# Router logits with tokens in partitions: which side of the matmul is stationary

## The chip, the core and the metric

The kernel runs on one core of a Trainium2 chip. The metric is the device time of one execution in microseconds (us). The core has TensorE (PE in the profile, PEld for its loads of the stationary operand), VectorE (DVE), ScalarE (ACT), GpSimd (POOL) and SyncE (SP), which run side by side and wait for each other through semaphores. TensorE writes to PSUM only; DVE and ACT read PSUM.

## The reference, cut to what matters

Two layers of a transformer-like trunk over 512 latent and 256 context tokens of width 1024; the second layer updates the latent tokens alone. Each layer is a block of token mixers and then a mixture of 16 experts. The router of that mixture is the place of the change:

```python
def grouped_moe(h, router_w, router_b, w1, w3, w2):
    logits = jnp.einsum('bld,de->ble', h, router_w, preferred_element_type=jnp.float32)
    s = jax.nn.sigmoid(logits)
    sb = s + router_b.astype(jnp.float32)
    grp = sb.reshape(sb.shape[:-1] + (N_EXPERT_GROUPS, EXPERTS_PER_GROUP))
    gscore = jnp.sum(lax.top_k(grp, GROUP_SCORE_TOPK)[0], axis=-1)
    gsel = jnp.argmax(gscore, axis=-1)
    ...
    _, idx = lax.top_k(jnp.where(in_group, sb, -jnp.inf), TOP_K)
    ...
    for e in range(N_EXPERTS):
        a = jax.nn.silu(h @ w1[e]) * (h @ w3[e])
        y = y + combine[..., e:e + 1] * (a @ w2[e])
```

`h` is (tokens, 1024), `router_w` is (1024, 16); everything is float32.

## The kernel before, in words

`trunk` writes one program by engine; a loop over the layer `l` holds, for each engine, its part of every stage, and named semaphores (`S(name)`, with the count that `at(name, l, n)` works out for layer `l`) set the order between the engines. `signals` holds how often each name is raised in a layer. `NT` is the number of tiles of 128 tokens: 6 in layer 0, 4 in layer 1. `KD` is 8, the number of 128-wide pieces of the model width; `NE` is 16.

The stretch around the change comes behind the output projection and ahead of the experts. In order:

- DVE writes the normed and modulated rows of a tile, tokens in partitions, to one of three buffers `h2tok` (L1961, L1962), two passes of 1024 columns a tile, and raises `h2_tok`. ACT stores these rows to memory (L1451), from where the experts later gather them.
- PE turns the tile in eight transposes of 128x128 (L997) into the PSUM pair `psb(t % 2)` and raises `h2_tr`. ACT copies the turned tile to `h2T[t % 2]` (L1455) and raises `h2T`. The copy of a tile waits until the logits of the tile two before are done.
- PE, one tile behind the transposes, multiplies: eight steps over the model width into `psb(3)[0:NE, ...]`, the router's weights `rwv` stationary (128 rows, 16 columns), the turned tile moving (128 columns). L1003 is that line. Each such float32 product shows as two matmuls in the trace, so 16 a tile. The logits lie with the experts in 16 partitions and the tokens along the columns.
- When all tiles are done, ACT copies the logits to SBUF (`lgT`, L1457), PE turns them back in `NT` small transposes into `psb(2)` (L1009), and ACT applies the sigmoid from there to `r_s` (L1459), now with the tokens in partitions. `route_sb` and `route_ps` carry these handovers.
- PE runs 45 transposes of the identity into a bank that nobody reads (`awake(3, 45)`, L1013, the line of the instruction is L653), then waits for DVE.
- DVE picks the two experts of each token from `r_s` (L1974 to L2002), PE counts the tokens of each expert (L1016, L1018), 55 more transposes of the identity follow, DVE works out blocks and places (L2015 to L2041), PE turns these into tables (L1027), 60 more transposes follow. With the expert numbers of the blocks (L2049) SP starts to load the experts' weights (L537, L591).
- The experts' blocks follow (L629 and others).

PE, ACT, DVE and SP each take their instructions in the order of the program text, so a wait holds up what stands behind it on the same engine.

Of the kernel before, what the change touches and what calls it, by code (L numbers as in the profile page):

```python
# [22 lines left out]
ACT = mybir.ActivationFunctionType  # L23
AX = mybir.AxisListType

P = 128
# [5 lines left out]
TOK = SEQ + CTX  # L32
LT = SEQ // P
AT = TOK // P
# [6 lines left out]
BC = BW // P  # L41
# [16 lines left out]
NE, NG = 16, 4  # L58
# [63 lines left out]
def signals(name):  # L122

    blocks = expert_blocks(TOK)
    rounds = H * ((2 * AT + 3) // 4)
    once = "g_scaled wT wT_tr"
    by_tile = ("cn cnT cn_tr h2T h2_tok h2_tr hT_hi hT_tile h_tok h_tr lg_ps n1_sq sgv sv_sq t_gain t_hrt t_qk "
               "t_sqd t_ss x_new n1_eps n1_rt pj t_sq t_eps t_rt h_aff")
    by_chunk = "cv_cu po_mix po_pl po_pp sgu_mix sgu_sum sgu_u"
    by_unit = "probs s_ps pv"  # L130
    by_head = "neg_tr neg_row o_sb"
    by_block = "aT_ps aT_sb aT_lo a_sb h1_ps h_ps put sil y_ps y_sb"
    counts = {
        **dict.fromkeys(once.split(), 1), "route": 4, "route_ps": 3, "route_sb": 2, "sum_eps": 2, "sum_rt": 2, **dict.fromkeys(by_tile.split(), AT), **dict.fromkeys(by_chunk.split(), BC),
        **dict.fromkeys(by_unit.split(), H * len(score_units(AT))), **dict.fromkeys(by_head.split(), H),
        **dict.fromkeys(("mx_ps", "negmax"), H * AT), "o_n": BC, **dict.fromkeys(by_block.split(), blocks),
        **dict.fromkeys(("g_prod", "g_ps", "g_sig"), 4 * KD), **dict.fromkeys(("qkT", "qk_hi", "qk_tr"), rounds),
        **dict.fromkeys(("idx", "xT_ps", "xgT", "xg_lo"), blocks + 1), **dict.fromkeys(("m_hi", "m_lo", "n2_sq", "w_sc", "w_tr", "w_x"), KD),
        **dict.fromkeys(("up_ps", "up_sb"), 4 * AT), **dict.fromkeys(("br_hi", "br_lo"), 4 * BC),
        **dict.fromkeys(("w_hi", "w_lo"), SPLITS), "prod": CHUNKS, "cv_evac": 2 * BC, "cv_y": BC, "po_pad": 1,  # L140

        "h2_st0": 16 * (AT // 3), "h2_st1": 16 * (AT // 3), "h2_st2": 16 * (AT // 3), "par_b": 16 * 2, "par_g": 32, "par_w": 16 * 3, "par_n2": 48,
        "par_g2": 16, "par_p": 16, "par_sb": 32, "x_back": 16 * AT,
        "xg0": 16 * (blocks // 2 + 1), "xg1": 16 * ((blocks + 1) // 2),
        "y_st0": 16 * ((blocks + 1) // 2), "y_st1": 16 * (blocks // 2), **{f"yg{j}": 32 * YPAIR.count(j) for j in range(3)},
    }
    return counts[name]
# [27 lines left out]
def trunk(nc, A, out):  # L175
# [6 lines left out]
    with ExitStack() as ctx:  # L182
# [20 lines left out]
        MGZ = place("MGZ", 2 * KD * TOK)  # L203
# [15 lines left out]
        ident = place("ident", P)  # L219
# [14 lines left out]
        def W(l):  # L234
            return TOK if l < DEPTH - 1 else SEQ
# [65 lines left out]
        def psb(i):  # L301
            return ps[:, i, :]
# [68 lines left out]
        h2T = [late[:, j * D:(j + 1) * D].rearrange("p (k t) -> p k t", k=KD) for j in range(2)]  # L371
# [37 lines left out]
        eid_i = place("eid_i", MAXB + 1, I32)  # L409
        tab_i = place("tab_i", MAXB + 1, I32)  # L410
        idx_i = [place(f"idx_i{j}", 1, I32) for j in range(2)]
        lgT = MGZ[0:NE, 0:TOK]

        NB = MAXB + 1
        ge_blk = MGZ[:, 0:2 * AT * (NB + 1)].rearrange("p (k t b) -> p k t b", k=2, t=AT)
# [6 lines left out]
        rwv = rw[:, :].rearrange("p (k e) -> p k e", k=KD)  # L422
# [18 lines left out]
        def S(name):  # L441
            if name not in sems:
                sems[name] = ctx.enter_context(nc.semaphore(name))
            return sems[name]

        def at(name, l, n):

            return n + (signals(name) if l else 0)
# [173 lines left out]
        def _(pe):  # L622
            mm = pe.matmul
# [43 lines left out]
            for l in range(DEPTH):  # L667
                NT = tiles(l)
# [59 lines left out]
                if l == 0:  # L728
                    pe.wait_ge(S("mod_row"), 1)
                    for k in range(KD):  # L730
# [3 lines left out]
                        for j in range(4):  # L734
                            last = mm(bank(4)[32 * j:32 * j + 2, 0:512], c_vec[:, k, :], mod_slot(k)[:, j * 512:(j + 1) * 512],
                                      start=(k == 0), stop=(k == KD - 1))
# [3 lines left out]
                for c in range(4):  # L740
                    last = pe.transpose(bank(7)[:, c * P:(c + 1) * P], mod_first[:, c * P:(c + 1) * P], ident[:, :])
# [161 lines left out]
                for j in range(4):  # L903
                    pe.wait_ge(S("w_lo"), split_no(l, S_V + j))
                    w = [a.rearrange("p (k n) -> p k n", n=BW) for a in parts(S_V + j, 2 * BW)]
                    for t in range(NT):
                        for i in range(2):
                            k, tok = 2 * j + i, slice(t * P, (t + 1) * P)
                            last = three(bank(t), (hH[:, k, tok], hL[:, k, tok]), (w[0][:, i, :], w[1][:, i, :]),
                                         BW, k == 0, k == KD - 1)  # L910
# [8 lines left out]
                for g in range(BC):  # L919
                    pe.wait_ge(S("sgu_u"), at("sgu_u", l, g + 1))  # L920
                    for t in range(NT):
                        last = mm(psb(home[g])[:, t * P:(t + 1) * P], sgv[:, t, g * P:(g + 1) * P], sguwT[:, g, :],
                                  start=True, stop=True)
# [5 lines left out]
                for c in range(BC):  # L929
                    for j in range(3):  # L930
# [8 lines left out]
                        last = chunk(l, S_CV + w, (hH, hL), w % 4)  # L939
                        if l == 0 and S_CV + w in rows_after:  # L940
                            last = half_turn(rows_after[S_CV + w], w % 4)
# [6 lines left out]
                for g in range(BC + 1):  # L948
# [9 lines left out]
                    if g >= 1:  # L958
# [4 lines left out]
                        last = mm(psb(2 + h % 2)[:, 0:SEQ], poolw[:, BC - 1 - h, :], pooled[h % 2][:, 0:SEQ], start=True, stop=True)  # L963
                        if W(l) > SEQ:
                            last = mm(psb(2 + h % 2)[:, SEQ:TOK], poolw[:, BC - 1 - h, :], pooled[h % 2][:, SEQ:TOK], start=True, stop=True)
# [7 lines left out]
                for n in range(KD + 1):  # L973
# [5 lines left out]
                    if n >= 1:  # L979
# [4 lines left out]
                        for t in range(NT):  # L984
                            last = pe.transpose(psb(2 + m % 2)[:, t * P:(t + 1) * P], wsc[m % 2][:, t * P:(t + 1) * P], ident[:, :])
# [5 lines left out]
                for t in range(NT + 1):  # L991
                    if t < NT:
                        pe.wait_ge(S("h2_tok"), at("h2_tok", l, t + 1))
                        if t >= 2:
                            pe.wait_ge(S("h2T"), at("h2T", l, t - 1))
                        for k in range(KD):
                            last = pe.transpose(psb(t % 2)[:, k * P:(k + 1) * P], h2tok[t % 3][:, k * P:(k + 1) * P], ident[:, :])  # L997
                        last.then_inc(S("h2_tr"), 1)
                    if t >= 1:
                        u = t - 1  # L1000
                        pe.wait_ge(S("h2T"), at("h2T", l, u + 1))
                        for k in range(KD):
                            last = mm(psb(3)[0:NE, u * P:(u + 1) * P], rwv[:, k, :], h2T[u % 2][:, k, :],  # L1003
                                      start=(k == 0), stop=(k == KD - 1))
                        last.then_inc(S("lg_ps"), 1)

                pe.wait_ge(S("route_sb"), at("route_sb", l, 1))
                for t in range(NT):
                    last = pe.transpose(psb(2)[:, t * NE:(t + 1) * NE], lgT[:, t * P:(t + 1) * P], ident[0:NE, 0:NE])  # L1009
                last.then_inc(S("route_ps"), 1)  # L1010


                awake(3, 45)  # L1013
                pe.wait_ge(S("route"), at("route", l, 1))
# [2 lines left out]
                for t in range(NT):  # L1017
                    last = mm(rank[:, t + 1:NT + 1, :], ones[:, :], r_any[:, t:t + 1, :].to_broadcast([P, NT - t, NE]),  # L1018
                              start=False, stop=(t == NT - 1))
# [5 lines left out]
                for i in range(2 * NT):  # L1025
                    k, t = i // NT, i % NT
                    last = mm(psb(3)[:, 0:2 * (nb + 1)].rearrange("p (s b) -> p s b", s=2), at_place[:, k, t, :],  # L1027
                              tab_blk[:, k, t, :, 0:nb + 1],
                              start=(i == 0), stop=(i == 2 * NT - 1))
# [73 lines left out]
        def _(act):  # L1103
            act_f = act.activation
# [20 lines left out]
            for l in range(DEPTH):  # L1125
                NT = tiles(l)
# [263 lines left out]
                for g in range(BC + 1):  # L1390
                    if g < BC:
# [3 lines left out]
                        last = act_f(pp[g % 2][:, PLL:PLL + SEQ], psb(g % 2)[:, 0:SEQ], ACT.Copy)  # L1395
                        if W(l) > SEQ:
                            last = act_f(pp[g % 2][:, PLC:PLC + CTX], psb(g % 2)[:, SEQ:TOK], ACT.Copy)
# [32 lines left out]
                for n in range(KD):  # L1430
# [4 lines left out]
                    last = act_f(wsc[n % 2][:, 0:SEQ], psb(n % 2)[:, 0:SEQ], ACT.Copy, scale=cw[:, g:g + 1])  # L1435
                    if W(l) > SEQ:
                        last = act_f(wsc[n % 2][:, SEQ:TOK], psb(n % 2)[:, SEQ:TOK], ACT.Copy, scale=cw[:, g + KD:g + KD + 1])
# [16 lines left out]
                        act.wait_ge(S("lg_ps"), at("lg_ps", l, t - 1))  # L1454
                    act_f(h2T[t % 2], psb(t % 2).rearrange("p (k t) -> p k t", k=KD), ACT.Copy).then_inc(S("h2T"), 1)  # L1455
                act.wait_ge(S("lg_ps"), at("lg_ps", l, NT))
                act_f(lgT[:, 0:W(l)], psb(3)[0:NE, 0:W(l)], ACT.Copy).then_inc(S("route_sb"), 1)  # L1457
                act.wait_ge(S("route_ps"), at("route_ps", l, 1))
                act_f(r_s[:, 0:NT, :], psb(2)[:, 0:NT * NE].rearrange("p (t e) -> p t e", t=NT), ACT.Sigmoid)\  # L1459
                    .then_inc(S("route_sb"), 1)  # L1460
                table(ACT.Silu)
# [78 lines left out]
        def _(dve):  # L1540
# [13 lines left out]
            for l in range(DEPTH):  # L1554
                NT = tiles(l)
# [304 lines left out]
                for c in range(BC):  # L1860
# [20 lines left out]
                    for a, b, o in cstreams:  # L1881
                        z = cvy[c % 2][:, o:o + b - a]
                        last = tt(z, z, gbs[c % 2][:, a:b], ALU.mult)
# [85 lines left out]

                    return a[:, :, None].to_broadcast([P, a.shape[1], n])  # L1970

                dve.wait_ge(S("route_sb"), at("route_sb", l, 2))
                dve.wait_ge(S("const"), 10)
                link(tt(sbv, s, rbias[:, None, :].to_broadcast([P, NT, NE]), ALU.add))  # L1974
                g3 = sbv.rearrange("p t (g e) -> p (t g) e", g=NG)
# [34 lines left out]
                    tt(gw[k][:, 0:NT], gw[k][:, 0:NT], r_den[:, 0:NT], ALU.mult)  # L2010

                nb = expert_blocks(W(l))
                dve.wait_ge(S("route_ps"), at("route_ps", l, 2))
                cnt = psb(2)[:, NT * NE:(NT + 1) * NE]
                link(tt(r_cnt, cnt[:, :, None].to_broadcast([P, NE, 6]), steps6[:, None, :].to_broadcast([P, NE, 6]), ALU.is_gt))  # L2015
                link(dve.tensor_reduce(r_nb, r_cnt, AX.X, ALU.add))
# [30 lines left out]
                link(dve.tensor_reduce(r_eid[:, 0:nb], blk, AX.X, ALU.add))  # L2047
                link(ts(r_eid[:, 0:nb], r_eid[:, 0:nb], float(NE - 1), None, ALU.min))
                cp(eid_i[:, 0:nb], r_eid[:, 0:nb]).then_inc(S("route"), 1)  # L2049
                dve.wait_ge(S("route_ps"), at("route_ps", l, 3))  # L2050
                code = psb(3)[:, 0:nb + 1]
                skip, half, dst = (a[:, 0:nb + 1] for a in (r_skip, r_half, r_dst))
                ts(half, code, YROWS + 0.5, float(-YROWS), ALU.is_gt, ALU.mult)
# [302 lines left out]
```

## Time and profile before

| | |
|---|---|
| Median of 3 runs | 2384.25 us (2383.99 to 2386.27) |
| Profiled execution | 2390.06 us, its span 2388.3 us |
| PE busy | 2142.1 us (90% of the span) |
| PE's weight loads busy | 1734.2 us (73%) |
| DVE, ACT, POOL busy | 1373.4, 992.8, 368.7 us |
| Granted PE clock, mean | 0.941 |
| The stretch of the change | about 1035 to 1056 us (layer 0), 2080 to 2096 us (layer 1) |

The span is the time from the first to the last instruction that the profiler shows; the execution's own time is 1.8 us longer, and lies 5.8 us above the median of the runs. The granted clock is the share of 2.4 GHz that TensorE was given; it has two levels in this trace, 1.00 and 0.50 (2.4 and 1.2 GHz). Matmuls overlap: the duration of one is longer than the distance to the next, so the cost of a sequence is read from the starts (or from the span of a group divided by its count), not from durations.

### The profile page before, as it was taken

How to read it: one execution, taken by the hardware profiler on the slowest of the kernel's cores; microseconds unless marked ns; L12 is line 12 of the kernel's file. 1: busy time of each engine (PE TensorE's matmuls, PEld its weight loads, DVE VectorE, ACT ScalarE, POOL GpSimd, SP SyncE). 2: the span in 40 equal slices, each digit the busy share in tenths (PEclk: the TensorE clock that was granted, in tenths of full speed). 3: DMA queues.
4: the chain of work that ended last, by engine and by line, in shares of the span. 5: the costliest groups of instructions: out<-in, count | busy, mean ns of one | idle time of the engine just before them, and what ended most of it. 6: DMA issues, size and time to landing. Idle time of an engine off the chain costs nothing.

```text
span 2388.3 us, 28736 instructions
## 1 busy us (share of the span) xinstructions
PE 2142.1 (90%) x10673; PEld 1734.2 (73%) x10673; DVE 1373.4 (58%) x1496; ACT 992.8 (42%) x1290; POOL 368.7 (15%) x400
## 2 busy tenths in 40 slices
PE   5879999899979999978999866999999989889994
PEld 3556787788768888867878654667788767778783
DVE  2646554755765433266888666453333454559885
ACT  3645412211211222225888655442422222338883
POOL 3300000000000001003555423000000000015552
PEclk7989999999989999998999987999999999999997
DMA  7020144444654232119999552003334343269994
GB/s 271 1 62 1 32 133 133 112 118 129 193 165 146 58 119 75 41 74 338 389 371 375 187 199 70 1 1 84 93 77 114 85 131 115 73 223 356 370 369 149
DMA packets 247398, 360.00 MB, mean 151 GB/s; under 512 B 22528, under 2 KB 180480, under 8 KB 245760
## 3 DMA queue, kind: packets, MB, share of 16 engines
q1 hardware_dynamic: 219776, 297.65, 38.2%
q0 software_dynamic: 22336, 42.07, 5.0%
q10 hardware_dynamic: 5184, 18.88, 2.0%
q8 instruction: 70, 1.15, 0.2%
q14 instruction: 32, 0.26, 0.0%
HBM read 354.23 MB, written 36.78 MB: 164 GB/s over the span
## 4 chain that ended last, share of the span: by engine, by line
PE 72%; DVE 11%; DMA 8%; ACT 5%; issue 3%; SPq 1%; POOL 0%; DVEq 0%; ACTq 0%; POOLq 0%
PE ps L639 33%; PE ps L629 17%; PE ps L641 8%; DMA RING<-in_moe_w 4%; PE ps L862 3%; DMA MGZ<-in_mod_w 2%; PE ps L1038 1%; PE ps L821 1%; PE ps L846 1%; PE ps L847 1%; DVE WS L1711 1%; PE ps L848 1%; ACT HTH L1484 1%; PE ps L810 1%; PE ps L1003 1%
## 5 line engine op out<-in xcount | busy, mean ns | idle before, releaser
L639 PE MATMUL ps<-HTH,WS 128*128 128x512 f32 x1664 | 587.4, 400 | 31.4 <-DVE WS L1711 13.2
L639 PEld LDWEIGHTS ps<-HTH,WS 128*128 128x128 f32 x1664 | 317.2, 191 | 109.6 <-issue 15.2
L639 PE MATMUL ps<-HTL,WS 128*128 128x512 f32 x832 | 330.2, 397 | 0.0
L629 PE MATMUL ps<-HTH,MGH 128*128 128x512 f32 x1000 | 283.4, 407 | 13.2 <-DVE MGH L2069 13.2
L1269 ACT ACTIVATE WS<-RAWB 128x1024 fp32r<-128x1024 f32 (+1 forms) x128 | 162.7, 1272 | 292.3 <-PE ps L641 97.0
L1711 DVE TENSOR_TENSOR WS<-RAWB,WS 128x1024 fp32r<-128x1024 f32 (+1 forms) x128 | 190.6, 1489 | 158.4 <-ACT WS L1269 158.3
L629 PE MATMUL ps<-HTL,MGH 128*128 128x512 f32 x800 | 232.4, 403 | 9.4 <-DVE HTL L2079 9.4
L641 PE MATMUL ps<-HTH,WS 128*128 128x256 f32 x832 | 235.7, 283 | 0.0
L629 PEld LDWEIGHTS ps<-HTH,MGH 128*128 128x128 f32 x1000 | 190.8, 195 | 55.8 <-DVE MGH L2069 8.9
L1484 ACT ACTIVATE HTH<-RING 128x2048 fp32r<-128x2048 f32 x100 | 191.2, 1912 | 82.3 <-DMA RING<-in_moe_w 59.3
L639 PE MATMUL ps<-BRH,WS 128*128 128x512 f32 x512 | 183.4, 397 | 16.9 <-DVE BRL L1857 13.3
L639 PEld LDWEIGHTS ps<-HTL,WS 128*128 128x128 f32 x832 | 159.0, 191 | 36.5 <-issue 1.0
L629 PEld LDWEIGHTS ps<-HTL,MGH 128*128 128x128 f32 x800 | 149.7, 192 | 39.5 <-issue 9.7
L1754 DVE TENSOR_TENSOR T<-T,ps 128x768 f32<-128x768 f32 (+1 forms) x48 | 39.4, 821 | 228.6 <-PE ps L641 116.8
L1287 ACT ACTIVATE T<-ps 128x768 f32<-128x768 f32 (+1 forms) x64 | 45.1, 705 | 294.5 <-PE ps L641 183.1
L1723 DVE SCALAR_TENSOR_TENSOR MGZ<-MGZ,scP 128x1024 f32<-128x1024 f32 x112 | 139.1, 1280 | 42.2 <-DMA MGZ<-in_mod_w 41.2
L641 PEld LDWEIGHTS ps<-HTH,WS 128*128 128x128 f32 x832 | 159.9, 192 | 0.1
L2079 DVE TENSOR_TENSOR HTH<-RING,HTH 128x2048 fp32r<-128x2048 f32 x50 | 114.6, 2293 | 54.0 <-ACT HTH L1484 51.9
L2079 DVE TENSOR_TENSOR HTL<-RING,HTH 128x2048 fp32r<-128x2048 f32 x50 | 114.6, 2292 | 23.6 <-ACT HTH L1484 23.6
L639 PEld LDWEIGHTS ps<-BRH,WS 128*128 128x128 f32 x512 | 97.2, 190 | 40.2 <-DVE BRL L1857 14.0
L641 PE MATMUL ps<-HTL,WS 128*128 128x256 f32 x416 | 117.8, 283 | 0.0
L2079 DVE TENSOR_TENSOR HTL<-RING,HTL 128x2048 fp32r<-128x2048 f32 x50 | 114.2, 2283 | 5.7 <-ACT HTL L1490 5.7
(336 smaller groups left out, 3775.1 us busy)
## 6 DMA issues: line engine op xcount, KB each, us to landing
RING<-in_moe_w SPq DMA_DIRECT2D x300, 512.0 KB
RAWB<-in_w_in SPq DMA_DIRECT2D x112, 512.0 KB, 4.3
MGZ<-in_mod_w SPq DMA_DIRECT2D x80, 512.0 KB, 4.1
RAWB<-in_w_branch SPq DMA_DIRECT2D x64, 256.0 KB, 4.7
MGZ<-y_rows POOLq DMA_DIRECT2D x20, 512.0 KB, 6.8
RAWB<-in_w_o SPq DMA_DIRECT2D x16, 512.0 KB, 3.9
HTF<-in_mod_w SPq DMA_DIRECT2D x6, 1024.0 KB
h_rows<-BR ACTq DMA_DIRECT2D x10, 512.0 KB, 2.6
```

The source lines that it names most:

```text
L629: last = mm(out, a, b, start=(first and i == 0), stop=(stop and i == 2))
L639: last = mm(psb(pair)[:, 0:SEQ], a[:, k0 + k, :], b[:, k, 0:SEQ], start=go, stop=end)
L641: last = mm(psb(pair)[:, SEQ:TOK], a[:, k0 + k, :], b[:, k, SEQ:TOK], start=go, stop=end)
L810: last = pe.transpose(head_bank[0 if h else r][0:QK, (i % 4) * P:(i % 4 + 1) * P], src, ident[:, :])
L862: last = mm(bank(4 + h % 2), v_tile(u)[:, h // 2, v0:v0 + P], pt, start=(u == 0), stop=(u == AT - 1))
L1269: act_f(parts(s, words(s))[0], raw_slab(r, words(s)), ACT.Copy).then_inc(S("w_hi"), 1)
L1287: act_f(sig[u % 2][:, 0:W(l)], psb(u % 2)[:, 0:W(l)], ACT.Sigmoid).then_inc(S("g_sig"), 1)
L1484: act_f(up_hi[half], slot(n % SLOTS), ACT.Copy).then_inc(S("e_hi"), 1)
L1711: tt(lo, raw_slab(FIRST + s, words(s)), hi.bitcast(F32), ALU.subtract).then_inc(S("w_lo"), 1)
L1723: stt(acc, half_slot(n), c, acc, ALU.mult, ALU.add).then_inc(S("half_acc"), 1)
L1754: link(tt(prod[:, 0:W(l)], sig[u % 2][:, 0:W(l)], psb(2 + u % 2)[:, 0:W(l)], ALU.mult))
L2079: tt(lo, slot(n % SLOTS), hi.bitcast(F32), ALU.subtract).then_inc(S("e_lo"), 1)
```

## The change

The sides of the router's product are swapped. The turned tile is the stationary operand (128 columns, the tokens), the sixteen columns of the router's weights move, and the result lands in `psb(2)` with the tokens in partitions, 16 columns a tile. The copy L1457 with its buffer `lgT`, the back turns L1009 and the waits between them are gone. The sigmoid reads `psb(2)` as before. The counts of `route_sb` and `route_ps` go down by one each.

```diff
-        "route": 4, "route_ps": 3, "route_sb": 2,
+        "route": 4, "route_ps": 2, "route_sb": 1,
...
                         for k in range(KD):
-                            last = mm(psb(3)[0:NE, u * P:(u + 1) * P], rwv[:, k, :], h2T[u % 2][:, k, :],
+                            last = mm(psb(2)[:, u * NE:(u + 1) * NE], h2T[u % 2][:, k, :], rwv[:, k, :],
                                       start=(k == 0), stop=(k == KD - 1))
                         last.then_inc(S("lg_ps"), 1)
-
-                pe.wait_ge(S("route_sb"), at("route_sb", l, 1))
-                for t in range(NT):
-                    last = pe.transpose(psb(2)[:, t * NE:(t + 1) * NE], lgT[:, t * P:(t + 1) * P], ident[0:NE, 0:NE])
-                last.then_inc(S("route_ps"), 1)
...
                 act.wait_ge(S("lg_ps"), at("lg_ps", l, NT))
-                act_f(lgT[:, 0:W(l)], psb(3)[0:NE, 0:W(l)], ACT.Copy).then_inc(S("route_sb"), 1)
-                act.wait_ge(S("route_ps"), at("route_ps", l, 1))
                 act_f(r_s[:, 0:NT, :], psb(2)[:, 0:NT * NE].rearrange("p (t e) -> p t e", t=NT), ACT.Sigmoid)\
                     .then_inc(S("route_sb"), 1)
...
-                dve.wait_ge(S("route_sb"), at("route_sb", l, 2))
+                dve.wait_ge(S("route_sb"), at("route_sb", l, 1))
...
-                dve.wait_ge(S("route_ps"), at("route_ps", l, 2))
+                dve.wait_ge(S("route_ps"), at("route_ps", l, 1))
...
-                dve.wait_ge(S("route_ps"), at("route_ps", l, 3))
+                dve.wait_ge(S("route_ps"), at("route_ps", l, 2))
```

## Rows read from the trace of the kernel before

**Rows 1.** The page: its chain by engine; and the router's group among the PE lines.
```profile
span 2388.3 us, 28736 instructions
...
PE 72%; DVE 11%; DMA 8%; ACT 5%; issue 3%; SPq 1%; POOL 0%; DVEq 0%; ACTq 0%; POOLq 0%
...
L1003 PE MATMUL ps<-MGZ,rw 128*16 128x128 f32 x160 | 19.6, 279 | 0.0
```

**Rows 2.** Chain of waits, layer 0: start us, us, what; then ACT's wait.
```profile
1046.69 1.02 PE ps L997 x8
1047.72 1.85 PE ps L1003 x16
1049.57 1.02 PE ps L997 x8
1050.59 3.61 PE ps L1003 x32
1054.22 0.81 ACT MGZ L1457
1055.08 0.56 PE ps L1009 x6
1055.66 0.26 ACT BR L1459
...
1082.34 1.93 ACT L1484 ACTIVATE HTH<-RING 128x2048 fp32r<-128x2048 f32 x1 [24.92 <-DMA RING<-in_moe_w]
```

**Rows 3.** Timeline of the tile loop, layer 0: start us, us, engine, line.
```profile
1043.61 1.23 DVE L1962 TENSOR_TENSOR BR<-BR,HTF 128x1024 f32<-128x1024 f32 x1
1046.06 1.23 DVE L1962 TENSOR_TENSOR BR<-BR,HTF 128x1024 f32<-128x1024 f32 x1
1046.62 0.85 PEld L997 LDWEIGHTS ps<-ident,BR 128*128 128x128 f32 x8 [0.21 <-issue]
1047.76 1.02 ACT L1455 ACTIVATE MGZ<-ps 128x1024 f32<-128x1024 f32 x1 [1.85 <-PE ps L997]
1049.50 0.85 PEld L997 LDWEIGHTS ps<-ident,BR 128*128 128x128 f32 x8 [0.21 <-issue]
1050.52 3.38 PEld L1003 LDWEIGHTS ps<-MGZ,rw 128*16 128x16 f32 x32 [0.17 <-issue]
```

**Rows 4.** Timeline of layer 1 behind the last logits.
```profile
2095.13 0.59 ACT L1457 ACTIVATE MGZ<-ps 16x512 f32<-16x512 f32 x1 [2.57 <-PE ps L1003]
...
2096.22 0.22 ACT L1459 ACTIVATE BR<-ps 128x64 f32<-128x64 f32 x1 [0.51 <-PE ps L1009]
```

**Rows 5.** Timeline and groups by shape: few moving columns behind 128 stationary ones.
```profile
1062.68 1.42 PEld L1018 LDWEIGHTS ps<-BR,ones 128*128 128x128 f32 x12
2110.10 1.86 PEld L1027 LDWEIGHTS ps<-MGZ 128*128 128x128 f32 x16 [0.66 <-DVE MGZ L2041]
...
L1018 PE MATMUL ps<-BR,ones 128*128 128x96 f32 x2 | 0.4, 268 | 0.0
L1018 PE MATMUL ps<-BR,ones 128*128 128x16 f32 x1 | 0.3, 262 | 0.0
```

**Rows 6.** Timeline, layer 1: eight transposes at the lower clock.
```profile
2083.06 1.57 PEld L997 LDWEIGHTS ps<-ident,BR 128*128 128x128 f32 x8 [0.82 <-DVE BR L1962]
```

**Rows 7.** Windows: length; PE, PEld, DVE, ACT, POOL busy; granted clock; DMA.
```profile
1035.00:1038.50 3.50, 2.92 (x13) 2.55 (x14) 3.46 (x4) 1.02 (x1) 0.00 (x0) 0.50 0.42 171
1038.50:1042.00 3.50, 3.50 (x30) 2.78 (x29) 3.43 (x4) 1.02 (x1) 0.00 (x0) 0.99 0.67 272
1069.30:1072.70 3.40, 1.65 (x15) 1.41 (x14) 3.33 (x8) 0.00 (x0) 0.00 (x0) 1.00 0.00 0
1072.70:1076.10 3.40, 3.40 (x18) 3.40 (x18) 0.76 (x3) 0.00 (x0) 0.00 (x0) 0.50 0.16 42
1076.10:1079.50 3.40, 3.40 (x18) 3.40 (x18) 0.84 (x6) 0.00 (x0) 0.92 (x1) 0.50 0.82 229
1714.40:1717.80 3.40, 1.38 (x13) 1.19 (x11) 3.37 (x4) 0.44 (x1) 0.00 (x0) 1.00 0.24 45
1717.80:1721.20 3.40, 2.49 (x6) 2.02 (x7) 3.23 (x6) 1.21 (x3) 0.00 (x0) 0.50 0.74 214
2083.00:2086.40 3.40, 3.34 (x15) 2.58 (x16) 3.37 (x4) 1.72 (x2) 0.00 (x0) 0.50 0.41 166
2086.40:2089.80 3.40, 3.40 (x31) 2.77 (x29) 1.48 (x2) 1.02 (x1) 0.00 (x0) 0.99 0.44 180
```

**Rows 8.** Timeline: PE at the counting matmuls, layer 0 and layer 1.
```profile
1062.46 0.47 PE L1016 MATMUL ps<-BR,tri 128*128 128x112 f32 x2 [1.78 <-DVE BR L2002]
2102.34 0.45 PE L1016 MATMUL ps<-BR,tri 128*128 128x80 f32 x2 [1.10 <-DVE BR L2002]
```

More of the change, by code:

```diff
@@ L133, in signals @@
     counts = {
-        **dict.fromkeys(once.split(), 1), "route": 4, "route_ps": 3, "route_sb": 2, "sum_eps": 2, "sum_rt": 2, **dict.fromkeys(by_tile.split(), AT), **dict.fromkeys(by_chunk.split(), BC),
+        **dict.fromkeys(once.split(), 1), "route": 4, "route_ps": 2, "route_sb": 1, "sum_eps": 2, "sum_rt": 2, **dict.fromkeys(by_tile.split(), AT), **dict.fromkeys(by_chunk.split(), BC),
         **dict.fromkeys(by_unit.split(), H * len(score_units(AT))), **dict.fromkeys(by_head.split(), H),
@@ L411, in trunk @@
         idx_i = [place(f"idx_i{j}", 1, I32) for j in range(2)]
-        lgT = MGZ[0:NE, 0:TOK]
         NB = MAXB + 1
```

## The prediction

> **What bounds the kernel now.** I read the page first. TensorE (PE) carries 72% of the chain that ended last, and the group the change rewrites, the router matmuls of L1003, is 160 instructions and 19.6 us of PE time in a span of 2388.3 us [rows 1]. So the change can't be worth much by its own work. What decides is whether the router sits on the path, and what its matmuls do beside computing. The chain of waits says that it is on the path, in both layers [rows 2]: transposes of L997 (8 a tile), router matmuls of L1003 (16 a tile, each of the 8 k steps being two instructions), again transposes, without another engine between them; then ACT's copy (L1457), the ten back turns (L1009, six of them here), ACT's sigmoid (L1459), some seven us of DVE work, the read of the expert numbers on SP, and a wait for the experts' weights from memory. These weights are asked for only when DVE has finished the routing, and ACT sits idle for 24.92 us until they land. So a microsecond more or less before the sigmoid is a microsecond at the end; nothing behind it can take it up.
>
> In layer 0 the loop's period is 2.87 us (1046.62 to 1049.50), PE's own: 8 transposes and 16 matmuls, in which PE is always at work. DVE needs 2.45 us for a tile (1043.61 to 1046.06), ACT's copy 1.02 us. So PE is the bound of this loop, by 0.4 us a tile [rows 3].
>
> **Removed.** The copy L1457, the back turns L1009 and the two handovers. From the copy's start to the sigmoid's start: 1055.66 - 1054.22 = 1.44 us in layer 0 [rows 2], 2096.22 - 2095.13 = 1.09 us in layer 1 [rows 4]. What follows is late by nothing else: the sigmoid waits for the logits alone, and ACT's function table for it is called for before the loop. Gain 2.53 us, all on the path. DVE's waits only change their numbers. The logits go to the PSUM pair from which the sigmoid read before, and the 45 transposes that keep PE awake (L1013) start as soon as the last logits are issued; that costs the sigmoid nothing.
>
> **Changed: the router matmul with its sides swapped.** Before, the stationary tile has 16 columns and 128 columns move; after, 128 are stationary and 16 move. Count stays 16 a tile. Before, 32 of them take 3.38 us of weight loads, (3.38 - 0.10) / 31 = 0.106 us each [rows 3]. What a matmul with few moving columns behind a full stationary tile costs is shown by L1018: its twelve move 96, 80, 64, 48, 32 and 16 columns, two of each, and take (1.42 - 0.19) / 11 = 0.111 us each, with the same duration at 96 columns (268 ns) as at 16 (262 ns). L1027 gives (1.86 - 0.19) / 15 = 0.111 us at 48 columns [rows 5]. The spacing follows the stationary load, not the columns that move. With the clock as before the loop thus gets 0.005 us x 16 = 0.08 us a tile dearer, 0.8 us over the ten tiles. Bounds: 0.106 (no loss) and 0.128 (the chain's 1.02 us for eight L997 transposes behind a full stationary tile, handover included [rows 2]; +3.5 us over the ten tiles); I take 0.111, since L1018 has the very shape.
>
> The Trainium skill (TensorE: Matmul & The Clock Gate, "LDWEIGHTS (loading the stationary operand)") says that the load's time goes by the number of stationary columns, whatever the rows; that agrees in kind with the rows. Its "Back-to-back issue gap" would let a warm matmul of up to 64 columns follow after some 25 ns; by that alone the sixteen would take 0.4 us a tile, and the rows of L1018 speak against it.
>
> **Changed: what PE does between the transposes.** This is the term that I think decides. PE's clock has two levels, 2.4 GHz (granted 1.00) and 1.2 GHz (0.50). At the lower one a transpose costs (1.57 - 0.23) / 7 = 0.191 us instead of 0.107, and L1027's matmuls 3.40 / 18 = 0.19 us instead of 0.111 [rows 6, 7]. Where the clock turns is seen in the windows [rows 7]. It is at 0.50 when the loop starts in both layers, since PE idles before. In layer 0 it is up at 1038.5, after thirteen transposes. In layer 1 it is up at 2086.4, after eight transposes and some eight router matmuls of 128 columns. At about 1072.7 it falls, after transposes, a pause and the first L1027 matmuls. And then comes the telling stretch: from 1072.7 to 1076.1 PE issues 18 matmuls of L1027, full stationary tile, 56 moving columns, with PE and its weight load busy for 3.40 of 3.40 us, and the clock stays at 0.50. It is up at 1079.5, after a stretch filled mostly with transposes of 128 columns, at the same rate of 18. A PE that is never idle, but loads much and streams little, didn't get its clock back; L922 adds that thirteen 128-column matmuls and then a pause let it fall [rows 7]. After the change two thirds of the loop are matmuls that stream 16 columns behind a full load, a third is transposes. I expect that the clock falls soon after 1042 and, once down, stays down until the 45 transposes: at the low clock the loop streams less still.
>
> The skill's page says (same page, "Part 4: PE-mode transpose") that transposes don't count as PE being busy and don't bring the full clock. The row of 1038.5 contradicts it: nothing but transposes had run. By that rule the clock would fall yet sooner, with the same end.
>
> **The price of the low clock.** Layer 0: mm(0) still runs at the high clock; four tiles of transposes and five of matmuls don't. 32 x (0.191 - 0.107) = 2.7 us and 80 x (0.191 - 0.106) = 6.8 us: 9.5 us, and 0.08 for mm(0), less 1.44: +8.1 us. Layer 1: the trace of before has half of mm(0), two tiles of transposes and three of matmuls at the high clock: 8 x 0.085 + 16 x 0.084 + 48 x 0.085 = 6.1 us, less 1.09: +5.0; should the clock still come up for one tile (16 x 0.08 + 8 x 0.084 = 2.0), +3.0. I take +4.0. The keep-awake transposes start cold: seventeen or so at 0.191, the rest at 0.109, is 17 x 0.191 + 28 x 0.109 = 6.3 us, up to 7.5 if the rise comes later. They hide under the time from the sigmoid's start to L1016: 1062.46 - 1055.66 = 6.8 us in layer 0 and 2102.34 - 2096.22 = 6.1 us in layer 1 [rows 2, 4, 8]. Late by 0 to 0.7 and 0.2 to 1.4: +0.5 in all. PE is ahead of that in both cases today, with 1.78 and 1.10 us to spare [rows 8].
>
> Sum: 8.1 + 4.0 + 0.5 = +12.6 us. The profiled execution took 2390.06 us (span 2388.3, 1.8 us around it); 2402.7 for such a one. The median of the runs, 2384.25, lies 5.8 us lower: 2396.8.
>
> **Rivals.**
> (a) The clock holds. PE has no pause in the loop, and the transposes, at the high clock, may be enough. Then the end is 2.53 - 0.8 = 1.7 us earlier: 2382.5, not slower. It decides at the second tile: if the granted clock is 1.00 from 1042 to the sigmoid, this case holds. For it: in the loop of before the matmul had only 16 stationary columns and the clock still held; against it: L1027's stretch. The skill's page ("Why this matters for your kernels") asks for a PE kept busy without gaps, and by that rule the clock holds, since the loop has none; that would be this case.
> (b) The clock falls in one layer only, or comes back within the loop. Layer 0 alone: 8.1 - 1.0 = +7, 2391; layer 1 alone: 4.0 - 1.4 = +2.6, 2387.
> (c) The matmuls really become cheap. Then DVE is the bound, with 2.45 us a tile: the last h2 tile is there at 1047.3, transposes and copy end by 1049.6, logits by 1050.2 instead of 1054.2: -4 us, in layer 1 as much, with the 2.5 about -11: 2373. L1018 speaks against it.
> (d) The swap does not reach the path, because something beside it holds the routing (the store of h2 rows, the weights): no change, 2384. The chain shows no such wait.
>
> **Chances.** Forecast (low clock in both layers) 0.70, (a) 0.15, (b) 0.10, (c) 0.03, (d) 0.02. A measurement of this kernel can tell about 0.2%, 4.8 us, from no change. Faster: (c), 0.03. Same: (a), (d) and a part of (b), 0.21. Slower: 0.76. The likeliest case by itself spans 2393 (the fall one tile later, 8.1 - 2.0; layer 1 at +3.0; no late transposes: +9) to 2401 (layer 0 never rises, +1.4; layer 1 +5.0; 2.0 late: +16.5). It holds 0.70 at most, so the range goes down over (b) to (a): 2381.6 to 2401.
>
> **What would show it.** Granted clock 0.50 from about 1042 to the 45 transposes in layer 0, and through the loop of layer 1; period of the loop near 5 us instead of 2.87; weight loads of the router matmul 0.11 us apart while the clock is high and 0.19 when it is low; sigmoid directly behind the last logits, some 8 us later than before in layer 0; everything behind it shifted, not stretched. I would be wrong if the clock holds with 16 moving columns, that is if the load of a full stationary tile keeps it up.

## Result, and the profile after

Beside the kernel before, the first four executions of the changed kernel had a median of 2404.85 us (2398.26 to 2408.86) against 2384.8 us (2383.99 to 2386.27): ratio 1.0075, 95% interval 1.0052 to 1.0097. The change makes the kernel slower, by more than was forecast and past the end of the range.

The profiled execution took 2398.26 us, with a span of 2396.5 us. The page's first part and the two groups of the loop, from the profile of the changed kernel:

```profile
span 2396.5 us, 28714 instructions
...
PE 2156.0 (90%) x10663; PEld 1750.9 (73%) x10663; DVE 1373.2 (57%) x1496; ACT 991.8 (41%) x1288; POOL 372.9 (16%) x400
...
L1002 PE MATMUL ps<-rw,MGZ 128*128 128x16 f32 x160 | 32.0, 351 | 0.0
L996 PE MATMUL ps<-ident,BR 128*128 128x128 f32 x80 | 18.6, 410 | 15.0 <-DVE BR L1953 15.0
```

The router's line (L1002 now) stands at 32.0 us of PE time instead of 19.6 [rows 1], though it has the same 160 instructions. The chain of waits in layer 0 shows where (start us, us, what):

```profile
1041.34 0.92 PE ps L996 x8
1042.26 2.52 PE ps L1002 x16
1044.78 1.79 PE ps L996 x8
1046.57 3.23 PE ps L1002 x16
1049.79 1.79 PE ps L996 x8
1051.58 3.23 PE ps L1002 x16
1054.81 1.79 PE ps L996 x8
1056.59 6.65 PE ps L1002 x32
1063.55 0.27 DVE BR L1965
```

It is the chain of [rows 2] with the same links: transposes, router matmuls, transposes. But a tile takes 5.0 us (1044.78 to 1049.79) instead of 2.87, from the fourth tile's transposes on. The copy and the back turns are gone; DVE starts 0.3 us after the last matmul, with only ACT's sigmoid (at 1063.27) between them. The granted clock of that stretch is in the windows (length; PE, PEld, DVE, ACT, POOL busy; clock; DMA share and GB/s):

```profile
1035.50:1038.90 3.40, 2.98 (x14) 2.58 (x14) 3.33 (x4) 1.02 (x1) 0.00 (x0) 0.50 0.50 202
1039.80:1042.90 3.10, 3.10 (x30) 3.10 (x30) 3.07 (x4) 1.51 (x2) 0.00 (x0) 1.00 0.44 165
1043.00:1047.00 4.00, 4.00 (x21) 4.00 (x20) 3.92 (x4) 0.72 (x2) 0.00 (x0) 0.50 0.34 138
1059.00:1062.80 3.80, 3.80 (x19) 3.80 (x20) 0.00 (x0) 0.00 (x0) 0.00 (x0) 0.50 0.00 0
2101.00:2105.00 4.00, 4.00 (x21) 4.00 (x20) 0.00 (x0) 0.00 (x0) 0.00 (x0) 0.50 0.00 0
```

From 1043 to 1062.8, and again in layer 1 (last row), PE and its loads are busy for the whole of each window, and the clock is at 0.50. In [rows 7] it was at 0.99 from 1038.5 and 2086.4 on.

For all kernels below I took the same three marks from the timeline, each counted from the first tile's first transpose: start of the sigmoid, start of the counting matmuls (L1016 before), and the cast of the expert numbers (L2049 before), which SP waits for. A group of matmuls starts with its first weight load. The names in brackets are those of the runs. In the kernel before, layer 0: 1035.13 (first transpose), 1055.66, 1062.46 and 1073.35, so 20.53, 27.33 and 38.22.

| Kernel | layer 0: sigmoid, counting, numbers | layer 1: the same | loss at the numbers, both layers | median minus before |
|---|---|---|---|---|
| before | 20.53, 27.33, 38.22 | 15.55, 21.67, 30.65 | | |
| before, second trace (before_again) | 20.69, 27.50, 38.39 | 15.42, 21.54, 30.51 | 0.0 | 0.8 |
| changed | 27.96, 34.76, 45.64 | 21.07, 28.39, 37.24 | 14.0 | 20.1 |
| changed, second trace (after_again) | 31.09, 37.89, 48.78 | 21.07, 28.21, 37.08 | 17.0 | 15.7 |
| 128 columns (wide128) | 19.60, 26.40, 38.40 | 13.88, 20.01, 28.97 | -1.5 | -0.2 |
| 64 columns (wide64) | 21.13, 27.92, 38.81 | 15.73, 21.85, 30.82 | 0.8 | 2.0 |
| 32 columns (wide32) | 31.12, 37.92, 48.81 | 21.10, 28.48, 37.34 | 17.3 | 13.4 |
| changed, filled pause (after_pre) | 27.14, 33.94, 44.83 | 21.07, 28.36, 37.21 | 13.2 | 12.6 |
| 128 columns in layer 1 only (wide_l1) | 24.83, 31.63, 42.53 | 14.05, 20.18, 29.16 | 2.8 | 9.2 |
| 128 columns, filled pause (wide128_pre) | 19.38, 26.18, 38.19 | 14.05, 20.18, 29.15 | -1.5 | -3.7 |
| the same, longer keep-awake (wide128_long) | 19.38, 26.18, 37.08 | 14.06, 20.18, 29.15 | -2.6 | -2.2 |
| changed, 8 more transposes a tile (fill8) | 22.29, 29.10, 40.00 | 26.09, 32.77, 41.63 | 12.8 | 18.2 |
| the same, filled pause (fill8_pre) | 22.34, 29.74, 40.63 | 18.08, 24.21, 33.19 | 5.0 | 4.0 |

The last column compares medians of one job. The marks are of one execution, the medians of 4 to 12, and the executions of one and the same kernel lie far apart: 93 of the kernel before, over five jobs, went from 2373.44 to 2398.00 us with a median of 2386.4, and the twelve of wide128_pre, in one job, from 2370.38 to 2395.18. That is why the table's marks carry the argument, and the medians only confirm its size.

The traced executions show this too. Both of before lie above its median (2390.06 and 2390.45 us), both of the changed kernel below its own (2398.26 and 2398.13), so their times differ by 8 us where the marks differ by 14.0 and 17.0. What lies outside the two marked stretches took 2319.4 and 2319.8 us in the former, 2313.6 and 2310.5 in the latter, and 2311.9 to 2319.3 in the nine other traces. Whether the routing's delay is in part taken up there can't be told from traces that scatter so. The medians, 15.7 us apart in the larger sample, don't suggest it.

### The profile page after: what moved, and what is told of

Read it like the earlier page. It is cut to its first block, busy times and chain, and to the rows that moved or that the text cites. A ratio compares the mean times of both kernels' runs of the same rounds, so it can differ in the third digit from the quotient of the medians.

```text
span 2396.5 us, 28714 instructions
## 1 busy us (share of the span) xinstructions
PE 2156.0 (90%) x10663; PEld 1750.9 (73%) x10663; DVE 1373.2 (57%) x1496; ACT 991.8 (41%) x1288; POOL 372.9 (16%) x400
## 3 DMA queue, kind: packets, MB, share of 16 engines
q8 instruction: 70, 1.15, 0.2%
## 4 chain that ended last, share of the span: by engine, by line
PE 72%; DVE 11%; DMA 9%; ACT 5%; issue 3%; SPq 1%; POOL 0%; DVEq 0%; ACTq 0%; POOLq 0%
PE ps L638 32%; PE ps L628 15%; PE ps L640 8%; DMA RING<-in_moe_w 4%; PE ps L861 3%; DMA MGZ<-in_mod_w 3%; PE ps L1002 1%; PE ps L1031 1%; PE ps L820 1%; PE ps L718 1%; DVE WS L1702 1%; PE ps L845 1%; PE ps L846 1%; PE ps L847 1%; PE ps L809 1%
## 5 line engine op out<-in xcount | busy, mean ns | idle before, releaser
L628 PE MATMUL ps<-HTH,MGH 128*128 128x512 f32 x1000 | 278.2, 400 | 12.7 <-DVE MGH L2060 11.9
```

The lines of the kernel that those rows point to most:

```text
L628: last = mm(out, a, b, start=(first and i == 0), stop=(stop and i == 2))
```

## Experiments

**The changed kernel again, and the kernel before again.** No edit.

> The changed kernel, unaltered, for a second trace and more times. Theory (the clock falls in the tile loop of both layers): the granted clock is 0.50 from the third or fourth tile to the keep-awake transposes in layer 0 and through the loop of layer 1, whatever the exact moment; sigmoid 6 to 9.5 us after that of before in layer 0 and some 5.5 us more in layer 1; median within 2398 to 2409. Open: the first trace shows some 14 us of loss in the two loops, the median of the runs 20; if that rest has a place, a trace of a slower execution shows it, either in the loops (clock never up in layer 0: 1.4 us more) or in a later stage.

Measured: 2400.37 us (7 executions, 2395.48 to 2407.63), ratio 1.0064 [1.0039, 1.0088], inside the forecast. The sigmoid of layer 0 came later than the 6 to 9.5 us that were forecast, by the case that was left open. Here the clock never came up in layer 0; PE alone in windows of its trace (length, PE busy, clock, DMA):

```profile
1036.00:1040.00 4.00, 4.00 (x20) 0.50 0.54 210
1040.00:1044.00 4.00, 4.00 (x21) 0.50 0.20 76
...
1060.00:1064.00 4.00, 4.00 (x20) 0.50 0.00 0
1064.00:1068.00 4.00, 4.00 (x23) 0.59 0.02 4
1068.00:1072.00 4.00, 3.46 (x32) 1.00 0.01 2
```

It rises only within the keep-awake transposes, which start at 1064.26. The sigmoid comes after 31.09 us, 10.6 later than before; the sigmoid of layer 1 repeats the first trace to the hundredth (21.07). So the loss varies with whether the clock comes up once at the start of layer 0: 14.0 and 17.0 us in the two traces. The seven executions here lie 15.7 us above the thirty of before in the same job, between the two. All eleven of the changed kernel have a median of 2401.05 us, so the 20 us of the first four look like a high draw; the two traces show no third place of loss, but neither is of one of the longest executions.

> The kernel before, unaltered, for a second trace. Its two loops should differ from the first trace's only by how long the start runs at the low clock: 19.5 to 21.5 us from first transpose to sigmoid in layer 0, 14.5 to 16.5 in layer 1, and the clock never falls inside them.

Measured: as expected, and the marks of the two traces of before differ by less than 0.2 us. Both traced executions took nearly the same time (2390.06 and 2390.45 us), so this doesn't say whether the spread between executions lies in this stage. In this job the fifteen others of before had a median of 2390.05 us, 5 above that of the first two jobs.

**The same matmul with 128, 64 and 32 moving columns.** The sixteen columns are read eight, four or two times over; loads, count, and the missing copy and back turns stay as in the changed kernel:

```diff
-                            last = mm(psb(2)[:, u * NE:(u + 1) * NE], h2T[u % 2][:, k, :], rwv[:, k, :],
+                            last = mm(psb(2)[:, u * P:u * P + 128].rearrange("p (c e) -> p c e", e=NE), h2T[u % 2][:, k, :],
+                                      rwv[:, k:k + 1, :].to_broadcast([P, 8, NE]),
                                       start=(k == 0), stop=(k == KD - 1))
```

This is the 128-column form. The sigmoid reads the first sixteen columns of each tile at their new places (that line is not shown).

> The changed kernel with one thing altered: the router's sixteen columns are read eight times over, so 128 columns move behind the same full stationary load; the same 16 instructions a tile, the same results in the first sixteen columns of each tile, copy and back turns still gone. Theory (few moving columns let the clock fall): clock at 1.00 through the loops once it is up, loop period 2.8 to 2.9 us, median 1 to 3 us below before, 2382 to 2384. Rival 1 (the full stationary load of 128 columns is what costs, by itself): the period stays near 5 us and the time near 2400. Rival 2 (the missing copy and back turns change something later, such as the DMA pattern or the keep-awake transposes): the loops are as fast as before, and yet the time stays 5 us or more above before.

> As wide128, with 64 moving columns (sixteen, four times over). Theory: spacing of the router's matmuls unchanged at 0.11 us while the clock is high; whether the clock holds is what is asked. If it holds, 2382 to 2385; if it falls, 2395 or more. The rival of the stationary load gives the same 2400 for 16, 64 and 128 columns.

> The changed kernel with 32 moving columns (the sixteen read twice). With 16 columns the clock fell and stayed down in both traces, with 64 and 128 it came up and held. Theory (few columns behind a full load let it fall): 32 columns are near 16, so the layer-0 loop from first transpose to sigmoid takes 27 to 31 us and the time is 2395 to 2401. Rival (anything above 16 holds the clock): 19.5 to 21 us for that loop and 2384 to 2388.

Measured: 2384.44 us for 128 (ratio 0.9994 [0.9978, 1.0011]), 2386.62 for 64 (1.0007 [0.9991, 1.0022]), 2399.24 for 32 (1.0059 [1.0034, 1.0084]). The times of 128 and 64 are 0.4 and 1.6 us above their forecasts and can't be told from before. Windows of PE in layer 0, first of 128 columns, then of 64, then two of 32 columns (one for each layer):

```profile
1032.50:1036.00 3.50, 3.08 (x14) 0.50 0.51 205
1036.00:1039.00 3.00, 3.00 (x18) 0.56 0.63 247
1039.20:1043.00 3.80, 3.80 (x37) 1.00 0.39 154
1043.00:1047.00 4.00, 4.00 (x39) 1.00 0.44 179
```
```profile
1040.40:1044.40 4.00, 4.00 (x22) 0.50 0.48 186
1044.40:1047.60 3.20, 3.20 (x22) 0.67 0.29 120
1047.70:1051.70 4.00, 4.00 (x40) 1.00 0.40 163
```
```profile
1044.00:1048.00 4.00, 4.00 (x21) 0.50 0.34 138
2093.00:2097.00 4.00, 4.00 (x21) 0.50 0.32 131
```

With 128 and 64 the clock comes up in the loop and stays; with 32 it stays at 0.50 like with 16 (31.12 us to the sigmoid, against 31.09). The stationary load is the same in all four. So the first rival, that the full load costs by itself, falls, and so does the second, that something behind the loop costs: wide128 lacks copy and back turns too. Nor is it the form of the edit, the repeated reading or the new places of the results, since the 32-column kernel has both and is as slow as the changed one. Adding columns whose results nobody reads makes the kernel 15.9 us faster than the changed one in the same job. The number of moving columns is the cause; each width has one trace, and the medians of 12, 12 and 6 executions agree with it.

The weight loads of the 128-column kernel, layer 0, also show what the swap does at the high clock:

```profile
1041.87 0.91 PEld L996 LDWEIGHTS ps<-ident,BR 128*128 128x128 f32 x8
1042.75 1.86 PEld L1002 LDWEIGHTS ps<-rw,MGZ 128*128 128x128 f32 x16
1044.53 0.91 PEld L996 LDWEIGHTS ps<-ident,BR 128*128 128x128 f32 x8
```

Period 2.66 us, not 2.87 (the forecast for this kernel was 2.8 to 2.9): the idle 0.17 and 0.21 us that stood before each group in [rows 3] are gone now that both kinds have 128 stationary columns. The sixteen are (1.86 - 0.19) / 15 = 0.111 us apart, as L1018 had said.

**Starting the loop at the high clock.** 55 transposes of the identity in PE's pause ahead of the tile loop:

```diff
+                awake(3, 55)
                 pe.wait_ge(S("w_x"), at("w_x", l, KD))
                 for t in range(NT + 1):
```

> The changed kernel, 16 moving columns, with 55 transposes of the identity ahead of the tile loop in both layers. Theory: the loop starts at the high clock and loses it within one or two tiles though PE is never idle; the last tiles run at 5.0 us each as before. First transpose to sigmoid 25 to 28 us in layer 0, 17 to 20 in layer 1; time 2392 to 2399. Rival (the clock only never came up, because the loop starts after a pause): clock 1.00 through the loops, 19 to 20 us in layer 0, time 2381 to 2384.

Measured: 2398.49 us (ratio 1.0045 [1.0024, 1.0067]). PE in layer 0:

```profile
1032.00:1036.00 4.00, 2.62 (x25) 1.00 0.55 163
1036.00:1040.00 4.00, 2.70 (x24) 1.00 0.54 220
1040.00:1042.80 2.80, 2.80 (x28) 0.98 0.59 238
1043.00:1047.00 4.00, 4.00 (x21) 0.50 0.32 131
```

The clock is at 1.00 when the loop starts and falls at about 1042.7, in the second tile's router matmuls, with PE busy without a gap from 1039 on. In layer 0 it isn't that the clock never got up; the loop loses it. Layer 1 is another case (PE alone):

```profile
2080.00:2084.00 4.00, 1.95 (x16) 0.97 0.33 132
2084.00:2088.00 4.00, 4.00 (x21) 0.50 0.59 240
```

There the clock falls at about 2083.7, where the second tile's transposes start behind PE's wait for DVE, and before the first router matmul (its load starts at 2085.24). The filled pause bought nothing: 21.07 us to the sigmoid, as in the changed kernel, where 17 to 20 were forecast. What the narrow matmuls do in layer 1 is to keep the clock from coming up again, which with 128 columns it does.

**One layer at a time.** 128 columns in layer 1 only (`if l == 1`), 16 in layer 0.

> The changed kernel with 128 moving columns in layer 1 alone, 16 in layer 0. Theory (a loss in each loop, 7.4 to 10.6 us in layer 0 and 6.4 to 6.6 in layer 1 up to the expert numbers, and nothing elsewhere): 7 to 11 us above before, 2392 to 2396, with layer 1 as in wide128 and layer 0 as in the changed kernel. Rival (the rest of the loss, that the first median showed beyond the two loops, has another place): more than 2398 although layer 1 is whole again.

Measured: 2395.06 us, ratio 1.0038 [1.0022, 1.0055], 9.2 above before. Layer 1 is that of the 128-column kernel (29.16 against 28.97). Layer 0 lost 4.3 us in this trace, since the clock held into the third tile's matmuls there. The median lies within the forecast and agrees with the two layers' loss being separate; the rival, more than 2398, is out.

**More streaming, 16 columns kept.** Eight transposes of the identity behind each tile's router matmuls, so that PE has more to do:

```diff
                         last.then_inc(S("lg_ps"), 1)
+                        if t < NT:
+                            awake(7, 8)
```

> The changed kernel, 16 moving columns, with eight transposes of the identity (128 columns, result unread) behind the router's matmuls of each tile, so PE has half as much again to do per tile. Theory (the clock needs columns that stream): once up, the clock holds, the period is 2.66 + 8 x 0.107 = 3.5 us instead of 5.0, layer 0 from first transpose to sigmoid takes 23 to 26 us, and the kernel is faster for the added work: 2388 to 2395. Rival (the sixteen-column matmul is itself slow, whatever runs beside it): each tile costs its 5.0 us and eight transposes more, over 32 us, and the time is above 2405.

Measured: 2408.26 us beside 2390.05, ratio 1.0096 [1.0060, 1.0132]. The forecast of the time was wrong. Of layer 0 the clock and the period came as forecast, and the sigmoid after 22.29 us, earlier than 23 to 26. PE in both layers of the one trace:

```profile
1044.00:1048.00 4.00, 4.00 (x39) 1.00 0.45 178
1056.00:1060.00 4.00, 4.00 (x39) 1.00 0.01 4
2088.00:2092.00 4.00, 4.00 (x22) 0.50 0.20 80
2100.00:2104.00 4.00, 4.00 (x21) 0.50 0.00 0
```

The same mix holds the high clock in layer 0, at 3.49 us a tile with half as much again to do, and sixteen 16-column matmuls are 0.111 us apart there ((1.86 - 0.19) / 15). So the 16-column matmul is not slow by itself. In layer 1 the mix never got the clock up, and each tile took 6.7 us. To ask whether the state at the start decides, the pause was filled here too:

> fill8 with 55 transposes of the identity in the pause ahead of the loop, so that the loop starts at the high clock in both layers. In fill8's trace the same mix of work held the high clock in layer 0 (period 3.49 us) and never got it up in layer 1 (period 6.7 us). Theory (the mix can hold the clock but not raise it; the state at the loop's start decides): now both layers hold it, periods 3.49 us, last logits 22 us after the first transpose in layer 0 and 15 in layer 1, time 2386 to 2392 beside a before of 2385. Rival (layer 1 differs for another reason): layer 1 stays at 0.50 and 6.7 us a tile, 25.9 us to the last logits, time above 2396.

Measured: 2391.66 us beside 2387.63, ratio 1.0031 [1.0000, 1.0061]. The time is inside the forecast, at its end. Layer 0 held until about 1056.5, in the last tile's router matmuls, some 1.3 us before the sigmoid; the keep-awake transposes then started at the low clock, and the expert numbers came 0.6 us later than in fill8. In layer 1 the clock fell in the first tiles, where PE still waits for DVE, and came up again inside the loop:

```profile
2076.00:2080.00 4.00, 2.00 (x17) 1.00 0.35 141
2080.00:2084.00 4.00, 3.96 (x21) 0.57 0.50 204
2084.00:2088.00 4.00, 4.00 (x24) 0.58 0.16 62
2088.00:2092.00 4.00, 4.00 (x39) 1.00 0.32 131
```

So the clock can come up in this mix and fall in it, against the theory as it was put. What decided in fill8's layer 1 stays open.

**A version that beats both?** 128 columns with the filled pause, and then with longer keep-awake stretches behind it (58 and 68 transposes instead of 45 and 55 in layer 0, 52 and 58 in layer 1):

> wide128 with 55 transposes of the identity in the PE pause of 7.6 us ahead of the tile loop, in both layers. Theory (PE is the loop's bound and starts it at the low clock): the first tiles run at the high clock; the first two are bounded by DVE, so little comes of it in layer 0 (about 0.5 us), about 1 to 1.5 us in layer 1, where the clock came up only within the third tile: 2380 to 2383. Rival (the clock comes up anyway before PE is the bound): no difference to wide128 within 1 us.

> wide128_pre with the keep-awake transposes that follow it made longer, 58 and 68 instead of 45 and 55 in layer 0, 52 and 58 in layer 1. In wide128 and wide128_pre the clock fell to 0.50 in the pause ahead of the counting matmuls in layer 0, and the expert numbers came 1.1 us later for it (12.0 us instead of 10.9 after the counting started). Theory: with the pause filled the counting runs at the high clock: 1 us less than wide128_pre in layer 0, 2379 to 2382. Rival (the transposes are now too long and hold up the counting): counting matmuls later than 26.5 us after the first transpose.

Measured: 2380.99 us (ratio 0.9986 [0.9963, 1.0008]) and 2383.72 us (0.9991 [0.9976, 1.0006]), the second above its forecast of 2379 to 2382. The filled pause moved the sigmoid of layer 0 by 0.22 us and layer 1 not at all (14.05 against 13.88), so the rival of wide128_pre was right. The loop did start at 1.00, but in both layers the clock fell at the second tile's transposes, behind PE's wait for DVE, and came up again inside the loop. PE in layer 1:

```profile
2076.00:2080.00 4.00, 3.25 (x30) 1.00 0.35 142
2080.00:2084.00 4.00, 2.70 (x15) 0.70 0.63 254
2088.00:2092.00 4.00, 4.00 (x38) 1.00 0.30 119
```

In wide128 and wide128_pre the clock was low at the counting matmuls of layer 0, and in wide128_long it was not; wide128 first, then wide128_long:

```profile
1058.96 2.52 PEld L1011 LDWEIGHTS ps<-BR,ones 128*128 128x128 f32 x12
```
```profile
1061.17 1.42 PEld L1012 LDWEIGHTS ps<-BR,ones 128*128 128x128 f32 x12
```

That gives the 1.1 us back (numbers at 37.08 instead of 38.19), and by its marks the kernel is 2.6 us ahead of before. Its interval includes 1.0: no version here is shown to be faster than before.

## Why the prediction was right or wrong

**The mechanism was right.** The router is on the path, and within the routing nothing takes up a delay: the counting follows the sigmoid by 6.80 us in layer 0 of both kernels, and in layer 0 the cast follows the counting by 10.89 and 10.88 us. The clock fell, the period near 5 us came (5.01), and the 128-column kernel shows that the few columns were what did it. Rival (a) held in neither trace of the changed kernel; (b) in neither; (c) is out, the spacing at the high clock is 0.111 us; (d) is out, the delay reaches the expert numbers in both layers.

**The removed part** was sized right in kind: in wide128 the sigmoid comes 0.93 us earlier in layer 0 and 1.67 in layer 1 (1.15 and 1.49 in wide128_long), where 1.44 - 0.48 and 1.09 - 0.32 were the sum with the dearer matmul. How late the clock comes up in each trace is in these numbers as well. A smaller step that failed is "the loop thus gets 0.08 us a tile dearer": the loop at the high clock got 0.21 us a tile cheaper, and the pauses between the groups went. The lower bound, 0.106 us an instruction, was no bound, because the gain lay between the groups.

**The price of the low clock was too small.** This is the step that failed, in two terms: layer 1, taken at +4.0 with at most 5.0, and the case "layer 0 never rises, +1.4".
- The matmul at the low clock was put at 0.19 us, from 18 instructions in a window of 3.40 us of [rows 7]. A window's count includes those that only reach into it. From starts and ends it is 0.214 us: sixteen loads in 3.54, the last of 0.333 us, (3.54 - 0.333) / 15:

```profile
1051.16 3.54 PEld L1002 LDWEIGHTS ps<-rw,MGZ 128*128 128x128 f32 x16
1054.43 1.76 PEld L996 LDWEIGHTS ps<-ident,BR 128*128 128x128 f32 x8
1056.17 6.95 PEld L1002 LDWEIGHTS ps<-rw,MGZ 128*128 128x128 f32 x32
```

  The transposes' 0.191 us was too low as well. The first two loads of a group behind a pause start only 0.06 us apart, and (1.57 - 0.23) / 7 of [rows 6] averages that in; from the second on the same group's loads start 0.213 us apart (2083.12 to 2084.40, six steps). The error is small in the sum, since the high clock's loop was underpriced too: a tile costs 5.01 - 2.87 = 2.14 us more, where 8 x 0.084 + 16 x 0.085 = 2.0 was reckoned, and the last 32 matmuls (1056.17 to 1062.86, against 3.6 us) 3.1 more instead of 2.7.
- Layer 0 was put at +8.1 with the clock up for mm(0). The first trace has +7.4 at the sigmoid, with the clock up a little longer. The second trace has +10.6: the clock never came up. The prediction knew this case ("layer 0 never rises, +1.4") and sized it at half: without it being up, mm(0), a group of transposes and half of mm(1) are at the low clock too, 3.1 us more than in the first trace.
- Layer 1 was put at +4.0, between 3.0 and 5.0. It is +5.5 at the sigmoid in both traces; the rise for one tile, for which 1 us was taken off, never came.
- The late keep-awake transposes were put at +0.5. They cost nothing in layer 0 and 1.2 us in layer 1 (counting 7.32 us behind the sigmoid instead of 6.12), within the stated 0.2 to 1.4.

Together 14.0 and 17.0 us at the expert numbers instead of 12.6, layer 1 with 6.6 and 6.4 of it; the 17.0 lie past the 16.5 from which the range's end was made. That is 1.4 to 4.4 of the 7.5 us by which the measured 20.05 us exceeds 12.6. **The rest is not located.** The range gave the scatter of the kernel itself no room: three executions of before within 2.3 us were taken as its spread, where 93 cover 25 us. With 15.7 us, the difference of the larger sample, the time would have been 2400 and inside. So the traces show that layer 1 lost more than forecast in both, and layer 0 in the second; that the median of four lay 3.85 us past the range's end looks to be in part the draw.

The sentence on the Trainium skill's rule (TensorE: Matmul & The Clock Gate, "Part 4: PE-mode transpose"), that transposes don't bring the full clock, is contradicted again: in the second trace of the changed kernel the clock rises from 0.50 to 1.00 in a stretch that holds nothing but transposes (1064.26 to 1070.7). The other rule that was weighed, of the same page ("Why this matters for your kernels"), that a PE kept busy without gaps keeps its clock, fails in layer 0 of the changed kernel: PE was busy for 3.10 of 3.10 us at 1.00 up to 1042.90 and for 4.00 of 4.00 us from 1043.00 on, and lost it between the two.

## What to carry to other kernels

Before swapping the sides of a small float32 matmul, count what streams as well as what is loaded: behind a full stationary load, few moving columns cost as much as many here (0.111 us each at 16 and at 128), and they may let TensorE's clock fall, or not come up, for everything around them. Where the moving side is narrow, reading it several times over cost nothing at the high clock and kept that clock in this loop (64 and 128 columns did, 16 and 32 didn't). Read the cost of a sequence from starts, never from a window's count, and give the range of a time the scatter of the kernel itself.

## What the runs showed that was not expected

- With 128 stationary columns in both, the groups follow each other without the 0.17 and 0.21 us pauses that stood between a 128-wide and a 16-wide group; the period at the high clock is 2.66 us instead of 2.87. That the unlike widths cause the pauses is likely and was not tried by itself.
- The same instruction mix (8 transposes, 16 narrow matmuls, 8 transposes) ran at the high clock in one layer and at the low one in the other layer of one execution, 3.49 against 6.7 us a tile. The time of such a kernel is a draw: fill8_pre went from 2385.18 to 2414.44 us.
- A loop that starts at 1.00 can lose it before its first router matmul: with the pause filled, the clock fell behind PE's first waits for DVE in layer 1 of after_pre and fill8_pre and in both layers of wide128_pre and wide128_long.
- The same kernel's executions lie up to 25 us apart, and the mean granted clock goes with it. Of the 89 executions of before with a clock on record, the 8 at 0.943 or less took 2392.2 us on average, the 12 at 0.950 or more 2380.6. The scatter is in other stages too: the loop of layer 0 started between 1032.35 and 1039.06 us in the thirteen traces, and from its expert numbers to the loop of layer 1 it took 999.7 to 1007.3 us. What sets it off wasn't tried.
